# A two-block network on one core: the small inner products of the gated recurrence taken in two runs, and the normalisation's product put ahead of its reciprocal

## The reference, cut to what matters

```python
# per layer: 256 tokens, 8 heads, key and value width 128
logf = log_sigmoid(z) + log1p(lb * exp(-z));  k = (1 - lb) * sigmoid(-z)
b = cumsum(logf, axis=tokens)
A[t, s] = sum_d q[t, d] * exp(b[t, d] - b[s, d]) * k[s, d]     # s <= t
o[t] = sum_s A[t, s] * v[s]
o = o * rsqrt(mean(o * o) + eps) * out_g ...                  # then gated, projected by w_out
x = layernorm(ALPHA * x + mix @ w_out) = (x - mu) * rsqrt(var + eps) * g + b
```

## Time and profile before

| | us |
|---|---|
| three runs of the kernel before | 1051.14, 1051.24, 1052.27 (median 1051.24) |
| the profiled execution, its own time | 1052.53 |
| its span, first to last instruction | 1050.7 |
| TensorE busy (matmul) | 1030.6 (98%) |
| VectorE busy | 730.9 (70%) |
| ScalarE busy | 654.1 (62%) |

### The profile page before, as it was taken

How to read it: one execution, slowest core, us unless ns; L and a number is a source line. 1 busy time by engine, 2 the same in 40 slices (tenths; PEclk the granted TensorE clock), 3 DMA queues, 4 the chain that set the end, 5 groups by cost and what they waited for, 6 DMA issues and landing times.

```text
span 1050.7 us, 19082 instructions
## 1 busy us (share of the span) xinstructions
PE 1030.6 (98%) x8048; PEld 922.0 (88%) x8048; DVE 730.9 (70%) x1085; ACT 654.1 (62%) x924; POOL 13.3 (1%) x18
## 2 busy tenths in 40 slices
PE   6999999999999999999999999999999999999996
PEld 5798987888989999988999998888799999988875
DVE  4684688885747788765565758977884656599686
ACT  6776576564456656544466678657755667776583
POOL 1000000000000000000000000100000000001000
PEclk9999999999999999999999999999999999999999
DMA  8663434666547655566544533422565455344231
GB/s 307 225 202 120 142 124 137 200 200 201 173 149 228 195 179 167 193 223 187 173 160 130 165 125 120 141 83 102 180 199 168 130 161 161 101 143 142 79 116 47
DMA packets 97831, 167.52 MB, mean 159 GB/s; under 512 B 7048, under 2 KB 32530, under 8 KB 97490
## 3 DMA queue, kind: packets, MB, share of 16 engines
q1 hardware_dynamic: 95776, 159.24, 47.3%
q0 software_dynamic: 1472, 5.51, 1.5%
q10 hardware_dynamic: 498, 1.55, 0.4%
HBM read 165.23 MB, written 1.05 MB: 158 GB/s over the span
## 4 chain that ended last, share of the span: by engine, by line
PE 95%; DVE 3%; DMA 1%; ACT 1%; issue 1%; SPq 0%; DVEq 0%
PE proj L598 13%; PE proj L589 13%; PE proj L600 13%; PE proj L599 13%; PE proj L591 13%; PE proj L590 13%; PE mix L935 1%; PE mix L979 1%; PE mix L936 1%; PE mix L634 1%; PE mix L659 1%; PE mix L642 1%; PE mix L968 1%; DVE wlo L1538 1%; DMA raw<-in_w_mem_kv 1%; PE mix L875 1%
## 5 line engine op out<-in xcount | busy, mean ns | idle before, releaser
L1538 DVE TENSOR_TENSOR wlo<-raw,whi 128x1024 fp32r<-128x1024 f32 (+3 forms) x303 | 355.4, 1202 | 139.9 <-ACT whi L1065 138.0
L1065 ACT ACTIVATE whi<-raw 128x1024 fp32r<-128x1024 f32 (+3 forms) x303 | 306.2, 1040 | 148.1 <-PE proj L600 66.5
L589 PE MATMUL proj<-act_hi,whi 128*128 128x256 f32 x1064 | 303.5, 285 | 0.6 <-ACT arena L1082 0.4
L591 PE MATMUL proj<-act_hi,wlo 128*128 128x256 f32 x1064 | 300.9, 283 | 0.0
L590 PE MATMUL proj<-act_lo,whi 128*128 128x256 f32 x1064 | 300.9, 283 | 0.0
L589 PEld LDWEIGHTS proj<-act_hi,whi 128*128 128x128 f32 x1064 | 203.1, 191 | 3.3 <-ACT arena L1082 1.2
L590 PEld LDWEIGHTS proj<-act_lo,whi 128*128 128x128 f32 x1064 | 203.2, 191 | 0.9
L591 PEld LDWEIGHTS proj<-act_hi,wlo 128*128 128x128 f32 x1064 | 203.2, 191 | 0.2
L598 PE MATMUL proj<-whi,y_hi 128*128 128x512 f32 (+1 forms) x340 | 135.1, 397 | 3.8 <-DVE wlo L1538 3.5
L599 PE MATMUL proj<-wlo,y_hi 128*128 128x512 f32 (+1 forms) x340 | 132.4, 389 | 0.0
L600 PE MATMUL proj<-whi,y_lo 128*128 128x512 f32 (+1 forms) x340 | 132.3, 389 | 0.0
(11 more groups left out here) (360 smaller groups left out, 1239.7 us busy)
## 6 DMA issues: line engine op xcount, KB each, us to landing
raw<-in_w_in SPq DMA_DIRECT2D x144, 512.0 KB, 4.4
raw<-in_w_up SPq DMA_DIRECT2D x88, 256.0 KB, 4.2
raw<-in_w_out SPq DMA_DIRECT2D x32, 512.0 KB, 4.3
raw<-in_w_down SPq DMA_DIRECT2D x22, 512.0 KB, 5.4
raw<-in_w_mem_kv SPq DMA_DIRECT2D x8, 512.0 KB, 9.1
raw<-in_w_mem_k SPq DMA_DIRECT2D x8, 512.0 KB, 4.0
raw<-in_w_o SPq DMA_DIRECT2D x8, 512.0 KB, 3.7
raw<-in_w_mem_v SPq DMA_DIRECT2D x8, 512.0 KB, 3.9
```

The source lines that it names most:

```text
L589: mm(o, wh[:, i, wc], hi[:, k0 + i, :], start=begin and j % 2 == 0, stop=False, skip_group_check=True)
L591: last = mm(o, wl[:, i, wc], hi[:, k0 + i, :], start=False, stop=end, skip_group_check=True)
L1065: fn(whi[c % SPLIT][:, 0:w], raw[c % SLOTS][:, 0:w], ACT.Copy).then_inc(s.w_hi, 1)
L1538: tt(wlo[c % SPLIT][:, 0:w], raw[c % SLOTS][:, 0:w], f32(whi[c % SPLIT][:, 0:w]), ALU.subtract).then_inc(s.w_lo, 1)
```

## The change

Four things are changed.

1. **The diagonal** (level 8, 16 small matmuls for each pair) goes from the odd unit into the even unit of the same pair, as its first run; level 3 of both heads comes last there as one run of 16. `keep` of an even unit writes one mask more, that of an odd unit one less.
2. **An odd unit's 64 small matmuls** are cut in two runs of 32: levels 4 and 5 (`early_products`) behind the first half of the next unit's decays, ahead of the gate piece; levels 6 and 7 (`late_products`) where `products` stood. For unit 7, the early run stands ahead of `outputs(2)` and the late run between the two token blocks of mlaout1's second piece.
3. **The waits.** The early run needs bank 2 of `mix` free, so the copies of levels 0 and 1 (`keep_widest`) are moved from `keep` into `factors` of the odd unit, between its second and third product, with a semaphore of their own (`hg_outer`); each product now signals alone. VectorE so waits for the even unit's products in the middle of the odd unit's factors. The wait for the cleared AT moves with the copies.
4. **In `normed`** the product (x - mu) * g is put ahead of the wait for the square root and the reciprocal.

The layout of the inputs is the same, and so is the number of matmuls. The diff's core:

```diff
 # TensorE
-                def products(u):
-                    pair, four = u // 2, u % 2
-                    pe.wait_ge(s.hg_z, 8 * L + u + 1)
+                def inner(u, levels):
                     low = 0 if u == UNITS - 1 else 2
...
+                def outer_products(u):
+                    pe.wait_ge(s.hg_z, 32 * L + 4 * u + 4)
+                    if u:
+                        pe.wait_ge(s.hg_cp, 8 * L + u)
+                    else:
+                        pe.wait_ge(s.hg_ll, 4 * L + 4)
+                    inner(u, (8,))
+                    Z = HZ[0]
+                    for hd in range(2):
...
+                    inner(u, (3,)).then_inc(s.hg_pr, 1)
+                def early_products(u):
+                    pe.wait_ge(s.hg_z, 32 * L + 4 * u + 2)
+                    pe.wait_ge(s.hg_outer, 4 * L + u // 2 + 1)
+                    inner(u, (4, 5))
+                def late_products(u):
+                    pe.wait_ge(s.hg_z, 32 * L + 4 * u + 4)
+                    pe.wait_ge(s.hg_cp, 8 * L + u)
+                    inner(u, (6, 7)).then_inc(s.hg_pr, 1)
...
                 for u in range(1, UNITS):
                     decays(u, 0, 2)
+                    if u % 2 == 0:
+                        early_products(u - 1)
                     if u < 4:
                         gates(u - 1)
...
-                    products(u - 1)
+                    if u % 2:
+                        outer_products(u - 1)
+                    else:
+                        late_products(u - 1)
...
+                early_products(UNITS - 1)
                 outputs(2)
-                products(UNITS - 1)
-                project("mlaout1", L, y_hi, y_lo, 8, part=(1, 2))
+                project("mlaout1", L, y_hi, y_lo, 8, part=(1, 2), amid=lambda: late_products(UNITS - 1))
 # VectorE
                     for i in range(4):
-                        last = halves(tt, u, i)
-                    last.then_inc(s.hg_z, 1)
+                        if u % 2 and i == 2:
+                            keep_widest(u - 1)
+                        halves(tt, u, i).then_inc(s.hg_z, 1)
+                def keep_widest(u):
+                    heads = slice(u, u + 2)
+                    dve.wait_ge(s.hg_pr, 8 * L + u + 1)
+                    if u == 0:
+                        dve.wait_ge(s.hg_zero, L + 1)
+                    copy(AT[:, heads, P:SEQ], mix[:, 2, 0:SEQ].rearrange("p (h t) -> p h t", h=2))
+                    copy(both(AT[0:64, heads, 64:P], SEQ, 64), mix[0:64, 2, SEQ:512].rearrange("p (h b t) -> p h b t", h=2, b=2)).then_inc(s.hg_outer, 1)
 # VectorE, normed
                     dve.wait_ge(s.ln_v, 2 * L + b + 1)
+                    stt(x, x, stat[:, 72 + 2 * b:73 + 2 * b], LNG, ALU.subtract, ALU.mult).then_inc(s.ln_s, 1)
                     dve.wait_ge(s.ln_r, 2 * L + b + 1)
                     nc.vector.reciprocal(r, r).then_inc(s.ln_s, 1)
-                    stt(x, x, stat[:, 72 + 2 * b:73 + 2 * b], LNG, ALU.subtract, ALU.mult).then_inc(s.ln_s, 1)
```

More of the change, by code:

```diff
@@ L286, in __init__ @@
         self.hg_cp = new("hg_cp")
+        self.hg_outer = new("hg_outer")
         self.hg_at = new("hg_at")
@@ L549, in _ @@
                 pool.wait_ge(s.hg_n, L + 1)
-                pool.wait_ge(s.hg_z, 8 * L + 1)
+                pool.wait_ge(s.hg_z, 32 * L + 4)
                 nc.gpsimd.memset(arena[:, 0:3584], 0.0).then_inc(s.hg_zero, 1)
@@ L559, in _, with project @@
             mm = nc.tensor.matmul
-            def project(name, L, hi, lo, tile0=0, ready=None, part=None, half=None):
+            def project(name, L, hi, lo, tile0=0, ready=None, part=None, half=None, amid=None):
                 g, ps, at = place[L, name], shape[L, name], number[L, name]
@@ L602, in project @@
                                 last.then_inc(half, 1)
+                            if amid is not None and b == 0:
+                                amid()
                     last.then_inc(s.w_used, 1)
@@ L948, in layer @@
                 project("hgi1", L, act_hi, act_lo, part=(3, 4))
-                def products(u):
-                    pair, four = u // 2, u % 2
-                    pe.wait_ge(s.hg_z, 8 * L + u + 1)
+                def inner(u, levels):
                     low = 0 if u == UNITS - 1 else 2
[L955 to L959, removed]
-                    for hd in range(2):
[L961 to L974, removed]
+                    for hd in range(2):
+                        h = 2 * (u // 2) + hd
+                        for l in levels:
+                            zk, zq = (HZ[u % 2][:, l % 4, hd, :],) * 2 if l < 8 else (HKT[:, h, :], HQT[:, h, :])
+                            at_bank, at = (3, (l // 8 + 1) * P) if l in (3, 8) else (low, (l - 4) * P)
                             at += hd * 64
@@ L979, in products @@
                                     last = mm(mix[32 * j:32 * j + 32, at_bank, at + 32 * b:at + 32 * b + 32], zk[:, t], zq[:, t], start=True, stop=True)
-                    last.then_inc(s.hg_pr, 1)
+                    return last
+                def outer_products(u):
[7 more added lines that the diff above has]
+                    for hd in range(2):
+                        z = Z[:, 0, hd, :]
+                        mm(mix[:, 2, hd * P:(hd + 1) * P], z[:, 0:P], z[:, P:SEQ], start=True, stop=True)
+                        for b in range(NB):
+                            z = Z[:, 1, hd, b * P:(b + 1) * P]
+                            at = SEQ + (2 * hd + b) * 64
+                            mm(mix[0:64, 2, at:at + 64], z[:, 0:64], z[:, 64:P], start=True, stop=True)
+                            z, at = Z[:, 2, hd, b * P:(b + 1) * P], (2 * hd + b) * 32
+                            for n in range(2):
+                                mm(mix[64 * n:64 * n + 32, 3, at:at + 32], z[:, 64 * n:64 * n + 32], z[:, 64 * n + 32:64 * n + 64], start=True, stop=True)
+                    inner(u, (3,)).then_inc(s.hg_pr, 1)
[7 more added lines that the diff above has]
+                    inner(u, (6, 7)).then_inc(s.hg_pr, 1)
                 def pair_bank(p):
@@ L2007, in keep @@
                     if u % 2 == 0:
-                        copy(AT[:, heads, P:SEQ], mix[:, 2, 0:SEQ].rearrange("p (h t) -> p h t", h=2))
-                        copy(both(AT[0:64, heads, 64:P], SEQ, 64), mix[0:64, 2, SEQ:512].rearrange("p (h b t) -> p h b t", h=2, b=2))
                         for n in range(2):
@@ L2012, in keep @@
                             copy(both(AT[rows, heads, 64 * n + 32:64 * n + 64], SEQ, 32), mix[rows, 3, 0:P].rearrange("p (h b t) -> p h b t", h=2, b=2))
-                        last = masked(3, mix[:, 3, P:2 * P])
+                        link(masked(3, mix[:, 3, P:2 * P]))
+                        last = masked(8, mix[:, 3, 2 * P:3 * P])
                     else:
@@ L2016, in keep @@
                         for l in range(4, 8):
-                            link(masked(l, mix[:, low, (l - 4) * P:(l - 3) * P]))
-                        last = masked(8, mix[:, low + 1, 0:P])
+                            last = masked(l, mix[:, low, (l - 4) * P:(l - 3) * P])
+                            if l < 7:
+                                link(last)
                     last.then_inc(s.hg_cp, 1)
```

1 line of the change is left out of this document (removed).

## The result

| | before | after |
|---|---|---|
| median of four runs (lowest to highest), us | 1051.47 (1051.14 to 1052.27) | 1061.45 (1060.11 to 1062.49) |
| ratio of the two | | 1.0085, 95% interval 1.0072 to 1.0098 |
| span of the profiled execution | 1050.7 | 1060.7 |
| TensorE busy | 1030.6 | 1038.0 |

The change makes the kernel 0.85% slower by the ratio, some 9 us (the two medians alone lie 10.0 apart), where I had said 0.45%. The direction was right, the size was outside the range.

The account below looks back on a forecast made before the run. TensorE, busy 1030.6 us of a 1050.7 span, was taken to bound the kernel. Layer 1 +3.0, layer 0 +1.7 and the tail -0.8 made +3.9 on the profiled 1052.53; forecast 1056.0, range 1051.4 to 1058.3.

Parts of the forecast that it names:

- Even units: Units taking the diagonal: 16 more small matmuls (0.30 us) and one new run end (0.20), +0.50 each, +2.00 a layer.
- Odd units: Units 1, 3, 5: 16 fewer small matmuls (-0.30 us) and one more run end (+0.19), -0.11 each, -0.33 a layer.
- Gates(4): First gate matmul of gates(4) loses 0.61 us to the SiLU; unit 3's early run fills this, -0.61 a layer.
- Outputs(0): VectorE, held inside factors(1), finishes the diagonal late; outputs(0) waits a little with its weight load exposed, +0.25 us a layer.
- The late run's margin at unit 1: Unit 1's late run starts at about 964.6, VectorE's masks are done at 964.4: no wait, by little.
- The last pair: Unit 6 to outputs(3): waits for VectorE's copies and the diagonal; +1.67 us in layer 1, +1.13 in layer 0.
- Supply of instructions: Layer 0's runs of units 3 and 7 lose 0.71 and 0.54 us to issue; shorter runs were taken not to starve.
- The tail: Last layer's normalisation behind TensorE: the product runs beside the square root, -0.4 us a block, -0.8 together.
- The sum: Layer 1 +3.0 us, layer 0 +1.7, tail -0.8: together +3.9 on the profiled execution's 1052.53; stated forecast 1056.0.
- no slower: Rival, chance 0.17: the two waits between unit 6 and outputs(3) don't open, 2.1 us less in each layer, 1051.8.
- starved runs are the rule: Rival, chance 0.11: without a profiler all eight odd runs lose 0.71 us; the cut gives back 5.7, so 1050.7.
- still slower: Rival, chance 0.10: VectorE falls behind through units 2 to 5, some 0.4 us in six places, both layers: 1058.5.

## Why the prediction was right or wrong

**What bounds the kernel** was read rightly: TensorE's own work and its waits. So were the direction, and the mechanism and length of each wait of the last pair. Step by step:

- **Even units**, "each even unit is +0.50": 0.59. The price of the new end, 0.20, is right. But "what is added is ends of runs" put a run's start at nothing, and it costs 0.09; dividing 1.49 by 80 had spread it over all matmuls. 0.4 a layer.
- **Odd units**, "-0.11 each": +0.11, for the same reason: two runs of 32 are 0.69 each, with their new end 1.58 against 1.49. 0.7 a layer with the wrong sign over three units; in unit 5 more, below.
- **Gates(4)**, "-0.61 a layer": -0.46 (the two stretches around unit 3 add up to -0.35, those around unit 1 without unit 0 to +0.11). The 0.61 rests on a misreading: the gate piece ends at 696.64, not at 696.5, so the four decays end at 697.57 and the first gate matmul, which ends at 698.14, lost 0.45.
- **What the shorter late run of unit 5 uncovers** was left out. I had seen the SiLU ahead of gates(4), and not the second one, ahead of mlaout1's first piece: TensorE's stretch behind the decays of u = 6 was its cover. From the start of their last matmul to that of mlaout1's first it took 3.71 before and 3.45 after, with some 0.9 less work in it. The late run of unit 5 gave back 0.16, where those of units 1 and 3 gave 0.69 and 0.79. This is the largest single omission, 0.5 a layer by the table and 0.66 by moving the early run into the wait.
- **Outputs(0)**, "+0.25": +0.21. `outputs(1)`, for which I had no term, is +0.10. **The late run's margin at unit 1** held.
- **The last pair**, idle 0.9 and 1.0, "+1.67": with unit 6's price taken out +2.27 in layer 1, of which 0.34, 0.77 and 1.16. The waits have the forecast's size; the rest is the starts of two runs (0.09 and 0.11) and a weight load and some signals around them.
- **Supply of instructions**, -1.25 in layer 0: measured -1.26 (4.08 against 5.34). The credit was right in size, and by luck in its reason: the gap sits at a fixed place of the stream and went with the diagonal's move alone, with runs of 64 uncut, so shorter runs weren't needed for it. In two kernels built on the changed one a gap came up in `outputs(2)`, right behind an early run of 32 (0.62 and 0.43). The Trainium skill (Runtime: NRT & Kernel Launch, Instruction fetch mechanics) says that fetching is hidden; the gap of 1.03 in the middle of a gate piece, at no wait, speaks against it.
- **The tail**, -0.8: -0.67.
- **The sum** was made of small prices, each counted many times, so that 0.1 too little in one of them came back eight or ten times. The start of a run at nothing is so the dearest step that failed: 1.0 a layer over the even and odd units and another 0.2 in the last pair, against 0.5 to 0.7 for the second SiLU. With 0.15 for gates(4), 0.1 for `outputs(1)` and the rest of the last pair, these are the 2.4 a layer by which the forecast was short. The range allowed 1 us for VectorE and none for TensorE's own prices being low.

Of the rivals, "no slower" fell with the last pair's two waits; "starved runs are the rule" fell too, since without those two layer 0 is the same as layer 1; "still slower" comes nearest in size (1058.5, measured 1061.45), but hasn't the cause: in the changed kernel VectorE held in the middle costs 0.2 at `outputs(0)` and then in the last pair only, and the added loss was TensorE's prices and a wait for ScalarE.

**Still open:** what sets the moment at which a packet of instructions starts and what fills the 1.3 us and more behind its end, and so how to order matmuls so that none is late; and whether the price of a change of width belongs to the stationary operand, to the moving one or to both.

## What to carry to other kernels

Order small matmuls by the width of their operands, over as many heads or blocks as the banks allow: each change of width cost 0.09 to 0.20 us here, and that order alone was worth 0.55%. Before cutting a run in two or moving a part of it ahead, list who waits at the end of the stretch that it leaves, not only who waits where it goes. A wait that guards a bank is worth a second look at which bank.

## What the runs showed of the hardware that was not expected

- A change of the operands' width, 128 to 64 to 32 and back, costs in both directions: four 64-wide matmuls took 1.04 together when each stood alone between others, and 0.61 in a row.
- TensorE's stream has stalls of 0.1 to 1.1 us that stay behind the same count of records whatever stands there. Six kernels had the one behind record 4781, and none of those with the diagonal moved, some of which had a gap elsewhere (0.4 to 0.8). Each stall ends 2.25 to 2.65 us behind the start of a 16 KB packet of the instruction queue.
- The granted clock fell to half for 3.4 us in ten of fourteen profiled executions, at about 186 us of the span, with TensorE (3.40 of 3.40 us), VectorE and ScalarE at work, and in one in the last pair too. At 186 us it costs 1.6 us: by so much the same matmuls come later behind it than ahead of it.
